# First microseconds: the first weights in two transfers, parameters on ScalarE's queue, part of the rounding on VectorE, x's first blocks in two PSUM buffers

## The chip, the cores and the metric

One core of one Trainium2 chip. The metric is the device time of one launch in microseconds (us). Engines: PE = TensorE, ACT = ScalarE, DVE = VectorE, POOL = GpSimd, SP = SyncE (it issues most DMA transfers here).

## The reference

A stack of four transformer-like layers, all in fp32, on x of 256 tokens by 1024 channels. What matters here is the very first step:

```python
def rms_norm(x, g):
    xf = x.astype(jnp.float32)
    y = xf * lax.rsqrt(jnp.mean(xf * xf, axis=-1, keepdims=True) + RMS_EPS)
    return (y * g.astype(jnp.float32)).astype(x.dtype)
...
    h = rms_norm(x, norm_mix_pre[layer])
    h = neighbourhood_attention(h, na_w_qkv[j], na_w_o[j], na_rpb[j])   # first: qkv = h @ w_qkv
```

Behind it come the output projection, a SwiGLU layer, dilated attention with a second SwiGLU layer, and twice a block of SwiGLU, four mixers (gated linear attention, forgetting attention, state space, short convolution) and SwiGLU. Nearly all the work is products with weight matrices of 1024 rows or columns.

## The kernel before, in words

The whole set of weights is laid out as a list of pieces, `w_all[m]`, each 128 partitions by 2048 columns (1 MB). SyncE fetches piece after piece into three raw buffers (`raw`). Each product is made in three fp32r products: ScalarE rounds the raw piece to fp32r (`wh`, the high part), VectorE subtracts (`wl` = raw - `wh`, the low part), and x is split in the same way into `xh` and `xl`. TensorE then adds `xh*wh`, `xl*wh` and `xh*wl` in PSUM. Low parts are ready later than high parts, so each piece's low products come last.

x comes in token rows and is needed with channels on the partitions. `turn(s, t, q)` does this for step s, token half t (128 tokens) and channel half q (four blocks of 128 channels). TensorE transposes four blocks of 128x128 into one PSUM buffer and signals once, behind the fourth (line 426, in `pe_program`). ScalarE waits for the signal and scales each block by the norm's gain, which is a column of the parameters `PR`, into `xh` (L1260). VectorE waits for ScalarE's fourth block and makes the four low parts `xl` (L1811). The factor of the norm itself is applied to the products later. The gains are in `PR`, which holds all small parameters (104 KB), and ScalarE waits for it before its first block.

At the start the values' projection of the first layer runs first (`values_start`), since its columns are in pieces 0 to 3. Piece 0 is treated apart: it comes in two transfers, columns 0 to 1023 (`s_first`) and 1024 to 2047 (`s_raw[0]`), and is rounded and subtracted in four pieces of 512 columns (`first_high`, L1238, and `first_low`, L1791). The issue order by hand is, on SyncE's queue: the identity (for transposes), the parameters, the first 1024 columns, x's second token half (512 KB), the second 1024 columns, pieces 1 and 2. On ScalarE's queue: x's first token half in two transfers of 256 KB, then the load of an activation table. TensorE waits for the identity, then does 7 filler transposes (`warm`), then `turn(0, 0, 0)`, `turn(0, 0, 1)`, 5 fillers, and `values_start`: the high products of channel block 0 for token half 0 (4 matmuls of 512 columns: `xh` with two column halves, `xl` with two), `turn(0, 1, 0)`, the low products of block 0 (2), high (4) and low (2) for token half 1, then block 1's (8 high), `turn(0, 1, 1)`, its 4 low ones, and piece 1. ScalarE's order is turn, first rounding (2), turn, turn, second rounding (2), piece 1. VectorE's is turn, first subtraction (2), turn, turn, second subtraction (2), piece 1. Each engine works in program order, and its waits are on semaphores.

Of the kernel before, what the change touches and what calls it, by code (L numbers as in the profile page):

```python
# [171 lines left out]
def build(nc, w_all, x_in, w_gu, cst, dist, prm, post, rpb, out):  # L172
    ctx = ExitStack()
    with ctx:
# [75 lines left out]
        s_first = signal("s_first", 16)  # L250
# [102 lines left out]
        def sp_program(e):  # L353
# [17 lines left out]
            q.on.dma_start(PR[:, :], prm).then_inc(*s_prm.up(0))  # L371
            q.on.dma_start(raw[0][:, 0:1024], w_all[0, :, 0:1024]).then_inc(*s_first.up(0))
# [37 lines left out]
        def pe_program(e):  # L410
# [10 lines left out]
            def turn(s, t, q):  # L421
                b = xbank(s, t, q)
                claim(b)
                t_.wait_ge(*(s_x[t][q * (1 - t)].of(0) if s == 0 else vx.of("x", s - 1, q, t)))
                for j in range(4):
                    k = t_.on.transpose(P[b][:, toks(j)], (xs if s else nx)[:, t, (4 * q + j) * 128:(4 * q + j + 1) * 128], ident)  # L426
                k.then_inc(*tx.up(("turn", s, t, q)))
                held[b] = [(vx, "lo", s, t, 4 * q + 3)]
# [325 lines left out]
            def values_start(banks):  # L754

                def high(m, i, t):
                    c = 2 * m + i
                    t_.wait_ge(*ax.of("hi", 0, t, c))
                    for x in (xh, xl):
                        for hf in range(2):  # L760
                            b = banks[t][hf]
                            if x is xl:
                                t_.wait_ge(*vx.of("lo", 0, t, c))
                            elif c == 0:
                                claim(b)
                            t_.wait_ge(*(hi.of(m) if m else hi.of(0, i, hf)))
                            mul(P[b][:, :], x[:, c, toks(t)], wh[m][:, (2 * i + hf) * 512:(2 * i + hf + 1) * 512],
                                x is xh and c == 0, False)
# [24 lines left out]
            def na():  # L793
                banks = ((2, 3), (4, 5))
                warm(2, 7)
                turn(0, 0, 0)
                turn(0, 0, 1)
                warm(2, 5)
# [421 lines left out]
        def act_program(e):  # L1220
# [13 lines left out]
            def first_high(i):  # L1234
                a.wait_ge(*(s_raw[0] if i else s_first).of(0))
                for hf in range(2):
                    n = slice(i * 1024 + hf * 512, i * 1024 + hf * 512 + 512)
                    a.on.activation(wh[0][:, n], raw[0][:, n], ACT.Copy).then_inc(*hi.up((0, i, hf), (0,)))  # L1238
                step["at"] = 1
# [14 lines left out]
            def turn(s, t, q):  # L1254
                b = xbank(s, t, q)
                name, l = GAINS[s]
                a.wait_ge(*tx.of("turn", s, t, q))
                for j in range(4):
                    c = 4 * q + j
                    a.on.activation(xh[:, c, toks(t)], P[b][:, toks(j)], ACT.Identity, bias=0.0,  # L1260
                                    scale=par(name, l, c)).then_inc(*ax.up(("hi", s, t, c)))
# [206 lines left out]
            def na():  # L1468
                turn(0, 0, 0)
                first_high(0)  # L1470
                turn(0, 0, 1)
# [276 lines left out]
            for h in range(2):  # L1748
                a.on.dma_start(nx[:, 0, halfs(h)], placed(0, halfs(h))).then_inc(*s_x[0][h].up(0))
            a.on.preload_act_table_set(LNEXP)  # L1750
# [12 lines left out]
        def dve_program(e):  # L1763
# [23 lines left out]
            def first_low(i):  # L1787
                for hf in range(2):
                    n = slice(i * 1024 + hf * 512, i * 1024 + hf * 512 + 512)
                    v.wait_ge(*hi.of(0, i, hf))  # L1790
# [14 lines left out]
            def turn(s, t, q):  # L1805
                b = xbank(s, t, q)
                name, l = GAINS[s]
                v.wait_ge(*ax.of("hi", s, t, 4 * q + 3))
                for j in range(4):
# [266 lines left out]
            def na():  # L2076
                turn(0, 0, 0)
# [514 lines left out]
        signals = s_raw + [s_first] + s_x[0] + s_x[1] + [s_ident, s_prm, s_cst, s_gu, s_dist] + s_rpb + [s_res, s_post] + s_out[0] + s_out[1]  # L2592
# [148 lines left out]
```

## Time and profile before

| | us |
|---|---|
| median of 3 runs | 1758.22 (1757.59 to 1758.23) |
| profiled execution, its own time | 1757.08 |
| its span, first to last instruction | 1755.3 |
| TensorE busy | 1747.8 |
| VectorE busy | 1226.1 |
| ScalarE busy | 987.8 |

The span leaves out what lies around the instructions (1757.08 less 1755.3). Busy time is a sum over an engine's instructions; ends of matmuls are modelled, so a busy TensorE is not one at its peak. Times in the trace count from the start of the span. 314.74 MB are moved, at 179 GB/s on average.

### The profile page before, as it was taken

What the parts mean: (1) busy time and instruction counts of PE and PEld (TensorE: products, weight loads), DVE (VectorE), ACT (ScalarE), POOL (GpSimd) and SP (SyncE); (2) the same over time, 40 slices, a digit from 0 to 9 for tenths busy, and PEclk for the clock granted to TensorE, in tenths of its full rate; (3) what the DMA queues carried; (4) which work ended last, traced back from release to release, by engine and by line L of the source; (5) the groups of instructions that cost most, each with busy time, mean ns of one, the idle gap of its engine ahead of it and who ended that gap; (6) DMA issues with size and microseconds to landing.
All of it is one profiled execution on the core that took longest, in us unless ns stands there. A gap on an engine that the chain in (4) does not pass through costs nothing.

```text
span 1755.3 us, 25579 instructions
## 1 busy us (share of the span) xinstructions
PE 1747.8 (100%) x10120; PEld 1499.3 (85%) x10120; DVE 1226.1 (70%) x1897; ACT 987.8 (56%) x1580; POOL 107.7 (6%) x191
## 2 busy tenths in 40 slices
PE   9999999999999999999999999999999999999999
PEld 7888888888888888888888888888888888888887
DVE  6877765667776777467756787775587648878763
ACT  6666554645555655365545666554565446656551
POOL 2000000701110000000001010000000001100000
PEclk9999999999999999999999999999999999999999
DMA  8435554554343455544454344555355534335552
GB/s 334 181 147 210 189 219 163 222 182 155 144 157 121 168 192 215 205 160 181 189 214 145 123 144 187 197 192 215 134 206 191 214 133 169 134 145 216 192 215 74
DMA packets 45353, 314.74 MB, mean 179 GB/s; under 512 B 5024, under 2 KB 5536, under 8 KB 8240
## 3 DMA queue, kind: packets, MB, share of 16 engines
q1 hardware_dynamic: 44912, 312.54, 47.8%
q8 instruction: 80, 1.31, 0.3%
q10 hardware_dynamic: 288, 0.52, 0.1%
q14 instruction: 41, 0.34, 0.0%
q0 software_dynamic: 32, 0.03, 0.0%
HBM read 312.03 MB, written 1.05 MB: 178 GB/s over the span
## 4 chain that ended last, share of the span: by engine, by line
PE 99%; DMA 0%; DVE 0%; ACT 0%; SPq 0%; issue 0%
PE P L419 96%; PE P L426 1%; PE P L718 1%; DMA raw<-w_all 0%; ACT xx L1260 0%; PE P L1058 0%; PE P L620 0%; PE P L1138 0%; DVE xx L1811 0%; PE P L1004 0%; DVE xs L1831 0%; PE P L1081 0%; PE P L952 0%; ACT wh L1238 0%; PE P L942 0%
## 5 line engine op out<-in xcount | busy, mean ns | idle before, releaser
L1776 DVE TENSOR_TENSOR wl<-raw,wh 128x2048 fp32r<-128x2048 f32 x287 | 656.8, 2294 | 186.9 <-ACT wh L1232 167.7
L1232 ACT ACTIVATE wh<-raw 128x2048 fp32r<-128x2048 f32 x291 | 551.8, 1900 | 191.3 <-PE P L419 170.6
L419 PE MATMUL P<-xx,wh 128*128 128x512 f32 (+2 forms) x2800 | 652.1, 385 | 0.0
L419 PEld LDWEIGHTS P<-xx,wh 128*128 128x128 f32 (+1 forms) x2800 | 503.1, 188 | 97.9 <-issue 1.7
L419 PEld LDWEIGHTS P<-xx,wl 128*128 128x128 f32 x2688 | 344.3, 191 | 12.4
L419 PE MATMUL P<-xx,wl 128*128 128x256 f32 x2688 | 350.7, 283 | 0.0
L1361 ACT ACTIVATE ft<-P 128x256 f32<-128x256 f32 x240 | 90.2, 382 | 231.8 <-PE P L419 231.8
L419 PE MATMUL P<-wh,fhh 128*128 128x512 f32 x528 | 206.2, 390 | 0.0
L419 PE MATMUL P<-wh,fhl 128*128 128x512 f32 x528 | 205.5, 389 | 0.0
L419 PE MATMUL P<-wl,fhh 128*128 128x512 f32 x528 | 205.5, 389 | 0.0
L1939 DVE TENSOR_TENSOR fg<-P,ft 128x256 f32<-128x256 f32 x240 | 101.8, 424 | 121.9 <-ACT ft L1361 116.7
L419 PE MATMUL P<-wh,xx 128*128 128x512 f32 x544 | 173.9, 395 | 0.9 <-ACT wh L1238 0.5
L419 PEld LDWEIGHTS P<-wh,xx 128*128 128x128 f32 x544 | 102.0, 188 | 23.1 <-issue 0.9
L419 PEld LDWEIGHTS P<-wh,fhl 128*128 128x128 f32 x528 | 99.1, 188 | 20.7
L419 PEld LDWEIGHTS P<-wh,fhh 128*128 128x128 f32 x528 | 99.1, 188 | 20.2
L419 PEld LDWEIGHTS P<-wl,fhh 128*128 128x128 f32 x528 | 99.2, 188 | 20.1
L419 PE MATMUL P<-wl,xx 128*128 128x512 f32 x272 | 104.3, 391 | 0.0
L1260 ACT ACTIVATE xx<-P,PR 128x128 fp32r<-128x128 f32 x160 | 45.1, 372 | 77.1 <-PE P L426 77.1
L1811 DVE SCALAR_TENSOR_TENSOR xx<-P,PR,xx 128x128 fp32r<-128x128 f32 x160 | 44.7, 344 | 58.1 <-ACT xx L1260 58.0
L2492 POOL TENSOR_TENSOR ss<-ss 128x2 f32<-128x2 f32 x10 | 2.0, 195 | 1147.0 <-ACT fsj L1265 903.7
L419 PE MATMUL P<-wh,dxp 128*128 128x512 f32 x192 | 61.2, 394 | 0.0
L1959 DVE TENSOR_TENSOR fh<-fs,fg 128x256 f32<-128x256 f32 x120 | 51.1, 426 | 13.9 <-DVE fg L1939 0.9
(326 smaller groups left out, 1468.3 us busy)
## 6 DMA issues: line engine op xcount, KB each, us to landing
raw<-w_all SPq DMA_DIRECT2D x289, 1024.0 KB, 4.8
nB<-rpb SPq DMA_DIRECT2D x4, 512.0 KB, 6.4
raw<-w_all SPq DMA_DIRECT2D x2, 512.0 KB, 6.5
xs<-x_in SPq DMA_DIRECT2D x1, 1024.0 KB, 7.7
fgb<-post SPq DMA_DIRECT2D x2, 512.0 KB, 6.2
out<-xs SPq DMA_DIRECT2D x4, 256.0 KB, 2.0
C<-cst SPq DMA_DIRECT2D x1, 769.0 KB, 8.4
ntm<-x_in ACTq DMA_DIRECT2D x2, 256.0 KB, 3.8
```

The lines of the kernel that those rows point to most:

```text
L419: return t_.on.matmul(o, l, r, start=start, stop=stop, skip_group_check=True)
L426: k = t_.on.transpose(P[b][:, toks(j)], (xs if s else nx)[:, t, (4 * q + j) * 128:(4 * q + j + 1) * 128], ident)
L718: k = t_.on.transpose(P[b][:, toks(place[c])], pA[h][:, toks(c)], ident)
L1232: a.on.activation(o, i, ACT.Copy).then_inc(*hi.up((m,)))
L1260: a.on.activation(xh[:, c, toks(t)], P[b][:, toks(j)], ACT.Identity, bias=0.0, scale=par(name, l, c)).then_inc(*ax.up(("hi", s, t, c)))
L1361: a.on.activation(AF["ft"][:, z, :], P[fbanks(s, j)[z]][:, S:2 * S], ACT.Copy).then_inc(*af.up(("side", s, j, z)))
L1776: v.on.tensor_tensor(o, i, h.bitcast(F32), ALU.subtract).then_inc(*lo.up(m))
L1811: v.on.scalar_tensor_tensor(xl[:, c, toks(t)], P[b][:, toks(j)], par(name, l, c), xh[:, c, toks(t)].bitcast(F32), ALU.mult, ALU.subtract). ...
L1939: v.on.tensor_tensor(fg[:, j % 2, z * S:z * S + S], P[fbanks(s, j)[z]][:, 0:S], AF["ft"][:, z, :], ALU.add).then_inc(*vf.up(("sum", s, j, z)))
L1959: v.on.tensor_tensor(fh[:, j % 3, :], sj, gj[:, S:2 * S], ALU.mult).then_inc(*vf.up(("h", s, j)))
L2492: g.on.tensor_tensor(ss[:, 4:6], ss[:, 0:2], ss[:, 2:4], ALU.add).then_inc(*gx.up(("sum", s)))
```

## The change

- SyncE issues the first 1024 columns of piece 0 as two transfers of 512 columns with a signal each, directly behind the identity.
- The parameters are issued by ScalarE's queue, behind x's two transfers and ahead of the table load.
- VectorE rounds columns 0 to 511 with a `tensor_copy` as its first instruction and signals it on its own semaphore (`lo`, name "first"). ScalarE rounds columns 512 to 1023 and later the second half of the piece, as before.
- The first `turn` is made in two: blocks 0 and 1 in PSUM buffer 6, as before, blocks 2 and 3 in buffer 1, each with its own signal. ScalarE's rounding of columns 512 to 1023 stands between the two. On VectorE both stand ahead of the first subtraction.
- The second row of fillers has 2 transposes, not 5.

```diff
--- before.py
+++ after.py
@@ -247,7 +247,7 @@
         P = [ctx.enter_context(nc.psum_tensor(f"P{i}", [128, 512], F32)) for i in range(8)]
 
         s_raw = [signal(f"s_raw{i}", 16) for i in range(RAW)]
-        s_first = signal("s_first", 16)
+        s_first = [signal(f"s_first{h}", 16) for h in range(2)]
         s_x = [[signal(f"s_x0{h}", 16) for h in range(2)], [signal("s_x1", 16)]]
         s_ident, s_prm, s_cst, s_gu, s_dist = (signal(n, 16) for n in ("s_ident", "s_prm", "s_cst", "s_gu", "s_dist"))
         s_res = signal("s_res", 16)
@@ -368,8 +368,8 @@
                 q.on.dma_start(gb, post[POST[s]:POST[s] + 1, :].broadcast_to([128, D])).then_inc(*s_post.up(s))
 
             q.on.dma_start(C[:, 0:128], cst[:, 0:128]).then_inc(*s_ident.up(0))
-            q.on.dma_start(PR[:, :], prm).then_inc(*s_prm.up(0))
-            q.on.dma_start(raw[0][:, 0:1024], w_all[0, :, 0:1024]).then_inc(*s_first.up(0))
+            for h in range(2):
+                q.on.dma_start(raw[0][:, halfs(h)], w_all[0, :, halfs(h)]).then_inc(*s_first[h].up(0))
             q.on.dma_start(nx[:, 1, :], placed(1, slice(0, D))).then_inc(*s_x[1][0].up(0))
             q.on.dma_start(raw[0][:, 1024:], w_all[0, :, 1024:]).then_inc(*s_raw[0].up(0))
             for m in range(1, RAW):
@@ -418,14 +418,14 @@
             def mul(o, l, r, start, stop):
                 return t_.on.matmul(o, l, r, start=start, stop=stop, skip_group_check=True)
 
-            def turn(s, t, q):
-                b = xbank(s, t, q)
+            def turn(s, t, q, js=(0, 1, 2, 3), b=None):
+                b = xbank(s, t, q) if b is None else b
                 claim(b)
                 t_.wait_ge(*(s_x[t][q * (1 - t)].of(0) if s == 0 else vx.of("x", s - 1, q, t)))
-                for j in range(4):
+                for j in js:
                     k = t_.on.transpose(P[b][:, toks(j)], (xs if s else nx)[:, t, (4 * q + j) * 128:(4 * q + j + 1) * 128], ident)
-                k.then_inc(*tx.up(("turn", s, t, q)))
-                held[b] = [(vx, "lo", s, t, 4 * q + 3)]
+                k.then_inc(*tx.up(("turn", s, t, q, js)))
+                held[b] = [(vx, "lo", s, t, 4 * q + js[-1])]
 
             def factors(s, b=6):
                 claim(b)
@@ -763,7 +763,7 @@
                                 t_.wait_ge(*vx.of("lo", 0, t, c))
                             elif c == 0:
                                 claim(b)
-                            t_.wait_ge(*(hi.of(m) if m else hi.of(0, i, hf)))
+                            t_.wait_ge(*(hi.of(m) if m else hi.of(0, i, hf) if i or hf else lo.of("first")))
                             mul(P[b][:, :], x[:, c, toks(t)], wh[m][:, (2 * i + hf) * 512:(2 * i + hf + 1) * 512],
                                 x is xh and c == 0, False)
 
@@ -793,9 +793,10 @@
             def na():
                 banks = ((2, 3), (4, 5))
                 warm(2, 7)
-                turn(0, 0, 0)
+                turn(0, 0, 0, (0, 1))
+                turn(0, 0, 0, (2, 3), 1)
                 turn(0, 0, 1)
-                warm(2, 5)
+                warm(2, 2)
                 values_start(banks)
                 for m in range(2, 4):
                     tok(0, m, 2 * m, banks)
@@ -1232,8 +1233,8 @@
                 a.on.activation(o, i, ACT.Copy).then_inc(*hi.up((m,)))
 
             def first_high(i):
-                a.wait_ge(*(s_raw[0] if i else s_first).of(0))
-                for hf in range(2):
+                a.wait_ge(*(s_raw[0] if i else s_first[1]).of(0))
+                for hf in range(1 - i, 2):
                     n = slice(i * 1024 + hf * 512, i * 1024 + hf * 512 + 512)
                     a.on.activation(wh[0][:, n], raw[0][:, n], ACT.Copy).then_inc(*hi.up((0, i, hf), (0,)))
                 step["at"] = 1
@@ -1251,11 +1252,11 @@
                     for t in range(2):
                         a.wait_ge(*ax.of("sq", s, h, t))
 
-            def turn(s, t, q):
-                b = xbank(s, t, q)
+            def turn(s, t, q, js=(0, 1, 2, 3), b=None):
+                b = xbank(s, t, q) if b is None else b
                 name, l = GAINS[s]
-                a.wait_ge(*tx.of("turn", s, t, q))
-                for j in range(4):
+                a.wait_ge(*tx.of("turn", s, t, q, js))
+                for j in js:
                     c = 4 * q + j
                     a.on.activation(xh[:, c, toks(t)], P[b][:, toks(j)], ACT.Identity, bias=0.0,
                                     scale=par(name, l, c)).then_inc(*ax.up(("hi", s, t, c)))
@@ -1466,8 +1467,9 @@
                 post_end(s, dbanks(s))
 
             def na():
-                turn(0, 0, 0)
+                turn(0, 0, 0, (0, 1))
                 first_high(0)
+                turn(0, 0, 0, (2, 3), 1)
                 turn(0, 0, 1)
                 turn(0, 1, 0)
                 first_high(1)
@@ -1747,6 +1749,7 @@
 
             for h in range(2):
                 a.on.dma_start(nx[:, 0, halfs(h)], placed(0, halfs(h))).then_inc(*s_x[0][h].up(0))
+            a.on.dma_start(PR[:, :], prm).then_inc(*s_prm.up(0))
             a.on.preload_act_table_set(LNEXP)
             a.wait_ge(*s_ident.of(0))
             a.wait_ge(*s_prm.of(0))
@@ -1787,7 +1790,7 @@
             def first_low(i):
                 for hf in range(2):
                     n = slice(i * 1024 + hf * 512, i * 1024 + hf * 512 + 512)
-                    v.wait_ge(*hi.of(0, i, hf))
+                    v.wait_ge(*(hi.of(0, i, hf) if i or hf else lo.of("first")))
                     v.on.tensor_tensor(wl[0][:, n], raw[0][:, n], wh[0][:, n].bitcast(F32),
                                        ALU.subtract).then_inc(*lo.up((0, i, hf), (0,)))
                 step["at"] = 1
@@ -1802,11 +1805,11 @@
                 v.wait_ge(*mm.of("half", s - 1, 1, 1))
                 v.wait_ge(*ax.of("sq", s, 1, 1))
 
-            def turn(s, t, q):
-                b = xbank(s, t, q)
+            def turn(s, t, q, js=(0, 1, 2, 3), b=None):
+                b = xbank(s, t, q) if b is None else b
                 name, l = GAINS[s]
-                v.wait_ge(*ax.of("hi", s, t, 4 * q + 3))
-                for j in range(4):
+                v.wait_ge(*ax.of("hi", s, t, 4 * q + js[-1]))
+                for j in js:
                     c = 4 * q + j
                     v.on.scalar_tensor_tensor(xl[:, c, toks(t)], P[b][:, toks(j)], par(name, l, c),
                                               xh[:, c, toks(t)].bitcast(F32), ALU.mult,
@@ -2074,7 +2077,10 @@
                 post_end(s, gb, tmp, dbanks(s))
 
             def na():
-                turn(0, 0, 0)
+                v.wait_ge(*s_first[0].of(0))
+                v.on.tensor_copy(wh[0][:, halfs(0)], raw[0][:, halfs(0)]).then_inc(*lo.up("first"))
+                turn(0, 0, 0, (0, 1))
+                turn(0, 0, 0, (2, 3), 1)
                 first_low(0)
                 turn(0, 0, 1)
                 turn(0, 1, 0)
@@ -2589,7 +2595,7 @@
                 means(s + 2)
 
 
-        signals = s_raw + [s_first] + s_x[0] + s_x[1] + [s_ident, s_prm, s_cst, s_gu, s_dist] + s_rpb + [s_res, s_post] + s_out[0] + s_out[1]
+        signals = s_raw + s_first + s_x[0] + s_x[1] + [s_ident, s_prm, s_cst, s_gu, s_dist] + s_rpb + [s_res, s_post] + s_out[0] + s_out[1]
         signals += [mm, tx, ta, th, hi, ax, aa, af, ah, lo, vx, va, vf, vh, gx, ga, gh]
         for program in (sp_program, act_program, dve_program, pool_program, pe_program):
             program(Still())
```

## Rows read from the trace of the kernel before

**Rows 1.** The page, busy time of TensorE (us, share of the span, instructions)

```profile
PE 1747.8 (100%) x10120; PEld 1499.3 (85%) x10120; DVE 1226.1 (70%) x1897; ACT 987.8 (56%) x1580; POOL 107.7 (6%) x191
```

**Rows 2.** The page, chain that ended last, shares of the span by engine

```profile
PE 99%; DMA 0%; DVE 0%; ACT 0%; SPq 0%; issue 0%
```

**Rows 3.** Waits of PE, whole span: engine, line, releaser: us, times, longest

```profile
PE P L752 <- DMA C<-cst: 2.5, 1, 2.5
PE P L419 <- ACT wh L1238: 0.5, 1, 0.5
PE P L419 <- DVE xx L1811: 0.4, 1, 0.4
```

**Rows 4.** Chain of the first 60 us: start, us, what

```profile
1.64 5.61 DMA raw<-w_all
...
9.91 1.16 ACT xx L1260 x4
...
11.09 0.36 DVE xx L1811
...
11.50 3.02 PE P L419 x12
```

**Rows 5.** Timeline of the issues: start, us, engine and line, operation, count

```profile
0.73 1.27 ACTq L1749 DMA_DIRECT2D ntm<-x_in  x2
1.18 0.42 SPq L371 DMA_DIRECT2D PR<-prm  x1
...
1.64 0.46 SPq L372 DMA_DIRECT2D raw<-w_all  x1
...
2.15 0.64 SPq L373 DMA_DIRECT2D ntm<-x_in  x1
```

**Rows 6.** DMA issues of 0.7 to 4.0 us: count, KB, us to landing

```profile
ntm<-x_in ACTq DMA_DIRECT2D x1, 256.0 KB, 3.7
...
PR<-prm SPq DMA_DIRECT2D x1, 104.0 KB, 3.4
...
raw<-w_all SPq DMA_DIRECT2D x1, 512.0 KB, 5.6
...
ntm<-x_in ACTq DMA_DIRECT2D x1, 256.0 KB, 3.9
...
ntm<-x_in SPq DMA_DIRECT2D x1, 512.0 KB, 6.8
...
raw<-w_all SPq DMA_DIRECT2D x1, 1024.0 KB, 9.1
```

**Rows 7.** Timeline of ScalarE

```profile
5.72 1.15 ACT L1260 ACTIVATE xx<-P,PR 128x128 fp32r<-128x128 f32 x4 [2.40 <-PE P L426]
...
7.27 1.15 ACT L1238 ACTIVATE wh<-raw 128x512 fp32r<-128x512 f32 x2 [0.40 <-DMA raw<-w_all]
...
12.64 1.92 ACT L1232 ACTIVATE wh<-raw 128x2048 fp32r<-128x2048 f32 x1 [0.54 <-DMA raw<-w_all]
```

**Rows 8.** Timeline of TensorE

```profile
2.55 1.76 PE L752 MATMUL P<-C 128*128 128x128 f32 x7 [2.55 <-DMA C<-cst]
...
4.49 1.98 PE L426 MATMUL P<-C,ntm 128*128 128x128 f32 x8 [0.18 <-DMA ntm<-x_in]
...
9.28 0.60 PE L426 MATMUL P<-C,ntm 128*128 128x128 f32 x4
...
15.73 3.82 PE L419 MATMUL P<-wh,xx 128*128 128x512 f32 x16
```

**Rows 9.** Timeline of VectorE, its first six instructions

```profile
7.02 1.12 DVE L1811 SCALAR_TENSOR_TENSOR xx<-P,PR,xx 128x128 fp32r<-128x128 f32 x4 [7.02 <-ACT xx L1260]
...
8.06 1.28 DVE L1791 TENSOR_TENSOR wl<-raw,wh 128x512 fp32r<-128x512 f32 x2
```

**Rows 10.** VectorE's groups of 0 to 60 us: busy, mean ns | idle before

```profile
L2089 DVE COPY nrb<-rb 128x256 f32<-128x256 f32 x1 | 0.7, 706 | 0.0
...
L2088 DVE TENSOR_SCALAR nrb<-rb 128x256 f32<-128x256 f32 x1 | 0.3, 294 | 0.0
```

## The prediction

> **What bounds the kernel now.** I read the page first. TensorE is busy for the whole span, 1747.8 of 1755.3 us [rows 1], and the chain that ended last is 99% TensorE [rows 2]. So almost nothing but TensorE's own work counts, and the change leaves that work as it is, apart from three filler transposes. Then the waits of TensorE over the whole run: beside 2.5 us for the identity at the start there are 0.5 us for rounded weights, 0.4 us for a low part of x, and nothing of size later [rows 3]. So there is no later stall that could swallow or enlarge a shift of the first microseconds. What the change can be worth is decided where TensorE stops waiting for the last time. The chain of the first 60 us gives that place: weights land at 7.25 (1.64 + 5.61), ScalarE rounds them, TensorE turns x's second token half from 9.28 on [rows 8], ScalarE scales it from 9.91 on, VectorE makes its low part at 11.09, TensorE goes on at 11.50 and does not stop again [rows 4]. I call 11.50 the last wait. A step that comes early ahead of it and does not move it is worth nothing.
>
> **The transfers.** Issues take their queue 0.4 to 0.6 us each. ScalarE's queue issues x's two halves of the first 128 tokens at 0.73 and about 1.38, ending at 2.00; SyncE's issues the parameters at 1.18, the first weights at 1.64, x's second token half at 2.15 [rows 5]. From issue to landing they take 3.7 and 3.9 us (x's halves: 4.43 and 1.38 + 3.9 = 5.28), 3.4 (parameters: 4.58), 5.6 (first weights: 7.25), 6.8 (second token half: 8.95) and 9.1 (piece 1: about 12.6) [rows 6]. After the change SyncE loses one issue (parameters, 0.42) and gains one (weights, about 0.46), so everything behind on its queue starts as before, and the bytes ahead of it are the same. The first 512 columns of the weights are issued at 1.18 and are half as large. They land between 4.9 (3.7 after issue, as the first 256 KB of x) and 7.25. The second 512 columns are issued at 1.64, with the identity, x, half the weights and perhaps the parameters before them. If the parameters' 104 KB come first, they land at 7.25 as now. If not, then earlier by 104/512 of the 1.97 us between x's landing at 5.28 and the weights' at 7.25, which is 0.4 us: 6.85. I take the middle, 7.05. The parameters become third on ScalarE's queue, at 2.00. From below 2.00 + 3.4 = 5.4; from above 2.00 + 6.8 = 8.8, the longest of the neighbours. I take the middle between x's 5.28 and the weights' 7.25: 6.3, against 4.58 now.
>
> **ScalarE.** Four scalings of x take 1.15 us, so they start 0.26 apart; two roundings take 1.15, 0.54 apart [rows 7]. x's first two blocks wait only for two transposes: TensorE starts at 4.49 and issues them 0.21 apart [rows 8], so they could be scaled from about 5.3 instead of 5.72. But they now wait for the parameters: 6.35, and ScalarE is free after two at 6.87. The gain of 0.4 us turns into a wait of 0.6, which costs nothing as long as ScalarE is free when the weights land, that is, while the parameters land before 6.48 (7.05 less two scalings, 0.52, and a pick-up of 0.05). Then the one rounding that stays here runs 7.07 to 7.70, the second pair of x's blocks starts at 7.61 and ends at 7.61 + 0.26 + 0.37 = 8.24, and x's blocks 4 to 7 run from 8.13 to 9.26. For the second token half ScalarE waits for TensorE, whose transposes wait for the landing at 8.95. They started at 9.28 before, behind matmuls that waited for the second rounding; those matmuls now end at about 8.6. So they start at 8.97, ScalarE at 9.60 instead of 9.91, and its fourth block is ready at 10.7 instead of 11.05. This is the only gain on the old chain: 0.3 us.
>
> **VectorE.** The new copy of 128x512 is not in the trace. From below it costs the 0.3 us that an operation with a constant takes for half that width, from above twice the slow 128x256 copy of 0.71, 1.4 us; I take 0.68, as the subtraction of this size (two in 1.28, 0.60 apart) [rows 9, 10]. If its weights land by 5.9 it is over by 6.6, and VectorE has nothing else before 6.9, as it now has nothing before 7.02: hidden, and at 1.4 us it is nearly so, since it idles again from 7.7 to 8.2. It frees ScalarE of 0.54 us. But behind it the order has changed. Before, the subtractions for the first weights began at 8.06, right behind the low parts of four blocks [rows 9]. Now the low parts of blocks 2 and 3 stand ahead of the subtractions on VectorE, and they wait for ScalarE's blocks, which stand behind the rounding, which waits for the weights: they start at 8.24 + 0.06 = 8.30. Then 2 x 0.26 = 0.52, two subtractions 2 x 0.60 = 1.20, blocks 4 to 7 4 x 0.26 = 1.04: 8.30 + 2.76 = 11.06 for the low part of the second token half. Before: 11.09. VectorE's queue takes the place of ScalarE's 10.7, and the 0.3 us won there is not collected.
>
> **TensorE.** Two PSUM buffers instead of one: the claim of the second is against a low part done at 9 us for a turn at 14.4, so it costs nothing. First matmul at about 6.8 instead of 8.05, the second at 7.75, subtractions' matmuls at 9.5 and 10.1. All of it ends before 11 and only adds idle time. After the last wait TensorE has the same work. What stands behind it as a floor: the 16 matmuls with piece 1's rounded weights start at 15.73 [rows 8], and its rounding starts at 12.64 on a transfer and takes 1.92 [rows 7], so it is ready at 14.56, and no shift beyond 1.17 us can pass.
>
> **The sum.** 11.06 against 11.09 is -0.03 us, to be read as none; with the weights at 7.25 it is +0.17, at 6.85 it is ended by ScalarE's 10.7 and gives -0.3. The profiled execution took 1757.08 us, 1.78 more than its span; the median of the runs is 1758.22, 1.14 above it, and the three differ by 0.64. I forecast 1758.2 and count 0.2%, 3.5 us, as what a measurement of this kernel tells from no change.
>
> **TensorE's clock.** The granted clock stands at full speed, 2.4 GHz, everywhere, yet the early transposes start 0.21 us apart up to 7.1 and 0.11 apart at 9.28 [rows 8]. I read that as the lower of the two levels, 1.2 GHz, in the first microseconds, not shown in the clock's row; the engine had worked almost without a gap from 2.55 to past 7 before it rose. Now the fillers end at about 6.6, and then come some eight matmuls in five microseconds. The Trainium skill, "TensorE: Matmul & The Clock Gate", Part 4 (PE-mode transpose), says that transposes do not count as TensorE being busy the way matmuls do. By that rule the dropped fillers cost nothing and the earlier first matmul would help. The trace speaks against it: at 9.28 only four matmuls had run, and the transposes were already at the fast spacing.
>
> **Rivals.** (A) *Transfers land earlier* (smaller ones, other order): weights by 6.7 and the second token half before 8.7. For it: the first weights are issued 0.46 earlier. Against: the same bytes are ahead. It gives 0.3 to 1.17 us, 1757.6. (B) *Parameters late*: they become the bound from a landing at 6.48 on, and from there each 0.1 us shifts ScalarE, VectorE and the last wait by 0.1. For it: they stand behind 512 KB of x on one queue and beside the weights on the other. At 7.25, with the weights, it is 7.25 + 0.57 - 7.05 = 0.77 late: 1759.0; at 8.8 it is 2.3 late: 1760.5. (C) *The clock rises later*, the slow side's worst: TensorE pauses too long after the shortened fillers and is at 1.2 GHz when the dense work begins at 11.5. Before, the climb took from 2.55 to between 7.1 and 9.28, 4.6 to 6.7 us. As long again at half rate loses half of it, 2.3 to 3.4 us: about 1761. It decides only if the low level outlasts 11.5; the slack before covers it. For it: fewer fillers, a gap at 6.6. Against: the engine kept the fast spacing at 9.28 after a wait of 0.5 us, and the wait of 0.4 us before 11.50 did it no harm [rows 3]. (D) *The split brings nothing*: the first 512 columns land with the rest at 7.25, VectorE's copy (0.68) ends at 7.95, still before its low parts of blocks 2 and 3 at 8.3; it gives the forecast's time, within 0.3.
>
> **Chances.** Forecast 0.50 (its own range 1757.9 to 1758.6), A 0.17, B 0.18, C 0.10, D 0.05. Only the edge of C with B on top passes 3.5 us: slower 0.03. No case gives a gain of 3.5 us; 0.02 for what I do not see; same 0.95. The range leaves out C (0.10) and some of B's and A's ends: 1757.0 (the floor of 1.17) to 1760.2.
>
> **What would show it.** Right: TensorE's first real matmul before 7, its last wait still near 11.5 and for VectorE's x, no idle time of VectorE between 8.3 and 11.4, ScalarE's first scaling at about 6.3 on the parameters, ScalarE idle before 9.6. Wrong: the last wait before 11.2 or after 11.8; weights' second half landing outside 6.85 to 7.25; transposes at about 9 still 0.21 apart and matmuls after 11.5 over 0.23 apart.

## The result, and the profile after

The changed kernel takes 1760.86 us in the median of 20 runs (1760.19 to 1761.38), the kernel before 1757.39 us in 20 runs beside it (1756.90 to 1758.94). The ratio is 1.0018, with a 95% interval of 1.0012 to 1.0024: 3.5 us slower. The profiled execution took 1761.38 us, 4.30 more than the one of before, with a span of 1759.6. It is the slowest of the 20 runs, 0.5 above their median, and the profiled one of before (1757.08) is 0.3 under its own, so the two traces show 0.8 us more than the medians do. One run of the kernel before, beside e9 to e12, took 6168.8 us and is left out everywhere.

The page of the changed kernel, busy time and the chain's shares by engine. TensorE's work is as before [rows 1, 2], but for three fillers. It is busy for 1.2 us more, from transposes and matmuls at a lower clock (below); the other 3.1 us of the longer span are waiting:

```profile
PE 1749.0 (99%) x10117; PEld 1500.0 (85%) x10117; DVE 1226.0 (70%) x1898; ACT 987.1 (56%) x1579; POOL 107.5 (6%) x191
...
PE 99%; DMA 0%; DVE 0%; ACT 0%; ACTq 0%; issue 0%; DVEq 0%
```

TensorE's waits (us in total, times, longest). The 2.4 us for x and the 1.8 us at the first real matmul are new [rows 3]:

```profile
PE P L426 <- DMA ntm<-x_in: 2.4, 1, 2.4
PE P L419 <- DVE wh L2081: 1.8, 1, 1.8
```

The chain of the first 60 us (start, us, what). Where the first weights stood [rows 4], the parameters stand now, for 8.32 us. The dense stretch, which began at 11.50, hangs on them and begins at 15.76 (inside the last line, which the view merges over the wait):

```profile
2.05 8.32 DMA PR<-prm
...
10.45 0.44 DVE wh L2081
...
11.03 2.26 PE P L419 x4
...
14.14 4.73 PE P L419 x16
```

The issues in their order (count, KB, us to landing), to be laid beside [rows 6]. x's halves land at 4.03 and at 1.4 + 6.2 = 7.6 (5.28 before), the weights' halves at 6.2 and 8.9 (7.25), the parameters at 2.05 + 8.3 = 10.4 (4.58), x's second token half at 10.55 (8.95):

```profile
ntm<-x_in ACTq DMA_DIRECT2D x1, 256.0 KB, 3.3
...
raw<-w_all SPq DMA_DIRECT2D x1, 256.0 KB, 5.0
...
ntm<-x_in ACTq DMA_DIRECT2D x1, 256.0 KB, 6.2
...
raw<-w_all SPq DMA_DIRECT2D x1, 256.0 KB, 7.3
...
PR<-prm ACTq DMA_DIRECT2D x1, 104.0 KB, 8.3
...
ntm<-x_in SPq DMA_DIRECT2D x1, 512.0 KB, 8.4
```

ScalarE and VectorE (start, us, line, operation, count, idle time before and who ended it). Both start at 10.45: ScalarE on the parameters, and VectorE's copy with it, though the copy's weights were there at 6.2. ScalarE had waited 6.47 us. VectorE's program begins with a wait for the parameters too (line 2466), ahead of the new copy. VectorE's idle time before its second token half, 0.37 us at 15.36, is a wait for ScalarE, which waited for TensorE at 14.18:

```profile
10.45 0.63 ACT L1261 ACTIVATE xx<-P,PR 128x128 fp32r<-128x128 f32 x2 [6.47 <-DMA PR<-prm]
10.45 0.43 DVE L2081 CAST wh<-raw 128x512 fp32r<-128x512 f32 x1 [10.45 <-DMA PR<-prm]
...
12.67 1.28 DVE L1794 TENSOR_TENSOR wl<-raw,wh 128x512 fp32r<-128x512 f32 x2
...
14.18 1.14 ACT L1261 ACTIVATE xx<-P,PR 128x128 fp32r<-128x128 f32 x4 [1.04 <-PE P L426]
...
15.36 1.13 DVE L1814 SCALAR_TENSOR_TENSOR xx<-P,PR,xx 128x128 fp32r<-128x128 f32 x4 [0.37 <-ACT xx L1261]
```

TensorE. The four transposes at 13.09 start 0.21 us apart, where those of [rows 8] at 9.28 started 0.11 apart, and of the four real matmuls at 14.79 the first two start 0.43 us apart, where the dense stretch of before has 0.23 [rows 8] (the other two follow the last wait, at 15.76):

```profile
7.67 1.12 PE L426 MATMUL P<-C,ntm 128*128 128x128 f32 x4 [2.39 <-DMA ntm<-x_in]
...
11.03 2.26 PE L419 MATMUL P<-wh,xx 128*128 128x512 f32 x4 [1.81 <-DVE wh L2081]
...
13.09 1.05 PE L426 MATMUL P<-C,ntm 128*128 128x128 f32 x4
...
14.79 1.77 PE L419 MATMUL P<-wh,xx 128*128 128x512 f32 x4
```

### The profile page after: what moved, and what is told of

Same layout as the page of the kernel before. It is cut to its first block, busy times and chain, and to the rows that moved or that the text cites. A ratio compares the mean times of both kernels' runs of the same rounds, so it can differ in the third digit from the quotient of the medians.

```text
span 1759.6 us, 25574 instructions
## 1 busy us (share of the span) xinstructions
PE 1749.0 (99%) x10117; PEld 1500.0 (85%) x10117; DVE 1226.0 (70%) x1898; ACT 987.1 (56%) x1579; POOL 107.5 (6%) x191
## 4 chain that ended last, share of the span: by engine, by line
PE 99%; DMA 0%; DVE 0%; ACT 0%; ACTq 0%; issue 0%; DVEq 0%
PE P L419 96%; PE P L426 1%; PE P L718 1%; DMA PR<-prm 0%; PE P L620 0%; PE P L1139 0%; PE P L1059 0%; ACT xx L1261 0%; DVE xx L1814 0%; PE P L1005 0%; DVE xs L1834 0%; ACTq L1751 0%; PE P L953 0%; PE P L1082 0%; PE P L943 0%
## 5 line engine op out<-in xcount | busy, mean ns | idle before, releaser
L1375 ACT ACTIVATE fs<-fg 128x256 f32<-128x256 f32 x120 | 49.7, 415 | 19.9 <-DVE fg L1955 16.6
```

The source lines that it names most:

```text
L1375: a.on.activation(fs[:, j % 2, :], fg[:, j % 2, 0:S], ACT.Silu).then_inc(*af.up(("s", s, j)))
```

## The experiments

"Before" in each is the kernel before, run beside it on the same chip: 1757.38 to 1757.45 us. Landings are counted from the start of the span, each in one trace. How far a landing moves by itself is seen in e2, e3, e8, e9 and e11, whose first transfers are the same: the parameters take 3.5 to 4.1 us, x's second half 4.0 to 4.5, the first 512 columns of the weights 4.4 to 5.1. A difference of 0.7 us or less between two traces says little.

**e1: only the parameters moved.**

```diff
-            q.on.dma_start(PR[:, :], prm)...          # SyncE, behind the identity
+            a.on.dma_start(PR[:, :], prm)...          # ScalarE, behind x's two transfers
```

> The kernel before, with the one edit that the parameters are issued third on ScalarE's queue. Theory 1 (the place behind x on that queue is what delays the parameters): they land 8 to 10.4 us into the span, ScalarE's first scaling waits for them, TensorE's dense stretch begins 3 to 4 us late and the time rises by 2.5 to 4 us. Theory 2 (the split of the weights into 2 KB rows slows all transfers): the parameters land by 6.5, the time rises by less than 1 us.

Measured: 1761.93 us, 4.5 above before (ratio 1.0025, 1.0014 to 1.0035). This one line costs at least as much as the whole change (the intervals overlap), and 0.5 more than the expectation's upper end: beside the late parameters, the second token half is turned 0.21 us per block at 13.66. Landings (x's second half, x's second token half, parameters), 7.7, 9.0 and 9.9:

```profile
ntm<-x_in ACTq DMA_DIRECT2D x1, 256.0 KB, 6.3
...
ntm<-x_in SPq DMA_DIRECT2D x1, 512.0 KB, 7.4
...
PR<-prm ACTq DMA_DIRECT2D x1, 104.0 KB, 7.9
```

Theory 1 holds. The weights here are one transfer with rows of 4 KB, so the split (theory 2) is not needed for the delay.

**e2: the changed kernel without that move.**

```diff
+            q.on.dma_start(PR[:, :], prm)...          # back behind the identity
-            a.on.dma_start(PR[:, :], prm)...
```

> The changed kernel, with the parameters back on SyncE's queue directly behind the identity. Theory 1: they land at about 4.6 again, the first real matmul is before 7.5, and the time is that of the kernel before or up to 0.5 us less. Theory 2: the weights' halves and x's second token half still land 1.5 us later than in the kernel before, and the time stays 1.5 to 2 us above it. Theory 3 (fewer fillers, lower clock at the dense stretch) gives at least 1 us above the kernel before, with matmuls more than 0.4 us apart past 10 us.

Measured: 1758.14 us, 0.7 above before (1.0003, 0.9993 to 1.0012), 2.7 below the changed kernel. The parameters land at 4.9, the first matmul is at 6.96. The timeline is the forecast's, step by step:

```profile
6.39 0.43 DVE L2081 CAST wh<-raw 128x512 fp32r<-128x512 f32 x1 [6.39 <-DMA raw<-w_all]
...
7.94 0.63 ACT L1240 ACTIVATE wh<-raw 128x512 fp32r<-128x512 f32 x1 [1.88 <-DMA raw<-w_all]
...
9.65 1.28 DVE L1794 TENSOR_TENSOR wl<-raw,wh 128x512 fp32r<-128x512 f32 x2
...
10.85 2.15 DVE L1814 SCALAR_TENSOR_TENSOR xx<-P,PR,xx 128x128 fp32r<-128x128 f32 x8
...
12.28 0.30 PEld L420 LDWEIGHTS P<-wh,xx 128*128 128x128 f32 x2 [0.77 <-DVE xx L1814]
```

VectorE rounds at 6.39, ScalarE rounds its half at 7.94 when it lands, VectorE's subtractions start at 9.65, its second token half follows without idle time, and the last wait ends at 12.28. That is 4.4 us behind the weights' landing at about 7.9, as the forecast's chain has it (7.05 to 11.06 for VectorE, plus 0.4 for TensorE's pick-up). The weights' second half landed 0.65 later than the whole did before, and it is issued 0.5 us later. Theory 3's case came by half: the median is not 1 us above.

**e3: only the split of the weights.**

```diff
+            for h in range(2):
+                q.on.dma_start(raw[0][:, halfs(h)], w_all[0, :, halfs(h)])...(s_first[h])
```

> The kernel before, with the one edit that the first 1024 columns of the weights come as two transfers with a signal each, on the queue's old place behind the parameters; ScalarE rounds both. Theory 1: landings move by under 0.3 us, the time is the same within 0.3 us. Theory 2: the second half, x's second token half and piece 1 land 1 us or more later than before, and the time rises by 1 to 1.7 us.

Measured: 1757.43 us against 1757.45 (0.9999, 0.999 to 1.0008). The split alone costs nothing and brings nothing that can be measured. The expectation had landings within 0.3 us, and that was a miss: in the trace x's second half lands at 5.8 (5.28 before) and piece 1 at 13.4 (12.6), with a last wait at 11.90, not 11.50.

**e4: 14 fillers in the changed kernel.**

```diff
-                warm(2, 2)
+                warm(2, 14)
```

> The changed kernel with 14 fillers, not 2, behind the turns, so that TensorE works from x's last turn to about the first real matmul. The parameters still land at about 10.4. If the low clock costs time (theory 3), the matmuls from 11 on are 0.23 us apart and the time falls by 0.4 to 1.2 us against the changed kernel. If the late parameters alone set the time, it moves by less than 0.2 us.

Measured: 1760.97 us, 0.1 above the changed kernel: no gain in the median. Yet in its trace the clock is up when it counts:

```profile
11.49 1.17 PE L419 MATMUL P<-wh,xx 128*128 128x512 f32 x4
...
12.50 0.60 PE L426 MATMUL P<-C,ntm 128*128 128x128 f32 x4
```

The four transposes at 12.50 start 0.11 apart, four matmuls at 11.49 take 1.17 us, and the last wait is at 14.98, not 15.76. Of these 0.8 us, 0.3 are the parameters' landing (ScalarE starts at 10.12, not 10.45), and 0.5 come behind it, where the transposes are faster and VectorE has no idle time before x's second token half. This profiled execution is 0.66 us shorter than that of the changed kernel, but the medians don't show it. How often the changed kernel runs into the lower clock late was not counted. Open.

**e5: the parameters on SyncE's queue, behind the first weights.**

```diff
-            q.on.dma_start(PR...); q.on.dma_start(raw[0][:, 0:1024]...)
+            q.on.dma_start(raw[0][:, 0:1024]...); q.on.dma_start(PR...)
```

> The kernel before, with the parameters on SyncE's queue still, but behind the first weights (512 KB) and not ahead of them. Theory S (what starves the parameters is ScalarE's queue: the transfer engines share between the two queues by packets, and SyncE's packets are larger and more): on SyncE's queue they land directly behind the weights, at 6.8 to 7.5, and the time rises by 0.7 to 1.3 us. Theory O (the order of issue is all: whatever is issued behind x and the weights waits for the whole backlog): they land at 8 or later and the time rises by over 2 us. By either, x's second half of the first 128 tokens lands at 7 or later, not at 5.3, since the weights are now issued 0.46 earlier beside it.

Measured: 1759.62 us, 2.2 above before. x's second half lands at 7.1, the parameters at 7.44. The landing is theory S's; the time is not (it had 0.7 to 1.3). In the trace the chain runs through x's second half, its turn and the five fillers to the first matmuls, at 9.3, so the time is not the parameters' alone. The profiled execution (1758.68) was this kernel's fastest:

```profile
PR<-prm SPq DMA_DIRECT2D x1, 104.0 KB, 5.8
```

**e6: parameters as in e1, and SyncE holds back what is behind the weights.**

```diff
             (SyncE, behind the first weights)
+            q.wait_ge(*s_prm.of(0))
             q.on.dma_start(nx[:, 1, :], ...)
```

> The parameters third on ScalarE's queue as in the first experiment, and SyncE waits for their landing before it issues x's second token half and all behind it. Theory S: what delays them is SyncE's transfers that are issued after them, so they land by 7, 3 us earlier than in the first experiment. Theory O: only what was issued before counts, so they land at 9 to 10 again. The time is no measure here, since x's second token half and piece 1 come 3 to 5 us later: 2 to 6 us above the kernel before.

Measured: the parameters land at 7.3, not 9.9; 1759.66 us, 2.3 above before and 2.3 *below* e1, although x's second token half is now issued at 7.36, 5.7 us later than in e1:

```profile
PR<-prm ACTq DMA_DIRECT2D x1, 104.0 KB, 5.3
```

So 2.6 us of e1's delay come from transfers of SyncE's queue other than the first weights: x's second token half, which e1 issues at 1.64, ahead of the parameters (2.03), and the rest, from 2.32 on, behind them. What stands behind is enough by itself: the changed kernel has the same bytes issued ahead of the parameters as e6 (the weights in two transfers), all else of SyncE's from 2.15 on behind them, and they land at 10.4. On SyncE's own queue (e5), with the same transfers behind, they land at 7.44.

**e7: the parameters first on ScalarE's queue.**

```diff
+            a.on.dma_start(PR[:, :], prm)...
             for h in range(2): a.on.dma_start(nx[:, 0, halfs(h)]...)
```

> The changed kernel with the parameters first on ScalarE's queue, ahead of x's two transfers. They should land at 3.5 to 4.5. Then VectorE's order sets the last wait by the forecast's formula, 4.4 us behind the landing of the weights' second half: with it at 7.5 to 9 the dense stretch starts at 12 to 13.4, 0.5 to 2 us above the kernel before. If x's second half lands after 8 (it is now third on its queue), ScalarE's blocks 4 to 7 are late too.

Measured: 1761.55 us, 4.2 above before (expected: 0.5 to 2). The parameters are there at 3.1, and x, issued 0.45 us later, is starved in their place: its first half lands at 1.2 + 7.9 = 9.1, its second at 11.0. My expectation for x was a miss:

```profile
PR<-prm ACTq DMA_DIRECT2D x1, 104.0 KB, 2.4
...
ntm<-x_in ACTq DMA_DIRECT2D x1, 256.0 KB, 7.9
```

**e8: e2 with VectorE's subtractions in their old place.**

```diff
-                turn(0, 0, 0, (2, 3), 1)
                 first_low(0)
+                turn(0, 0, 0, (2, 3), 1)
```

> The changed kernel with the parameters back on SyncE's queue (second experiment) and one more edit: on VectorE the first two subtractions stand ahead of the low parts of blocks 2 and 3, as they stood before the change. If VectorE's new order is what left that version 0.4 us (in the trace) to 0.7 us (in the runs) behind the kernel before, the last wait comes 0.4 to 0.5 us earlier relative to the landing of the weights' second half (3.9 us behind it, not 4.4) and the time falls to within 0.3 us of the kernel before. If not, it stays at 0.5 to 0.8 above.

Measured: 1758.32 us, but its runs go from 1756.67, under the fastest of before, to 1760.22. The time fell into neither case. The profiled one is of the lower clock, and its last wait comes 4.8 us behind the weights, not 3.9; TensorE turns x's second token half 0.21 us per block at 9.89, and ScalarE gets it at 10.98:

```profile
9.89 1.05 PE L427 MATMUL P<-C,ntm 128*128 128x128 f32 x4
...
10.98 1.14 ACT L1262 ACTIVATE xx<-P,PR 128x128 fp32r<-128x128 f32 x4 [1.05 <-PE P L427]
```

**e9: e8 with 7 fillers, not 2.**

```diff
-                warm(2, 2)
+                warm(2, 7)
```

> The changed kernel with the parameters on SyncE's queue, VectorE's first subtractions ahead of the low parts of blocks 2 and 3, and 7 fillers, not 2, behind the turns. Theory C (the early pause of TensorE leaves it at the lower clock and that is what holds the e8 version back): the matmuls from 8.4 on are 0.23 us apart, x's second token half is turned by 9.2, the last wait is at 11.3 to 11.8, and the time is 0.8 to 1.2 us below e8, that is 0.3 us below the kernel before to 0.1 above. Without theory C it stays 0.9 us above the kernel before.

Measured: 1757.45 us, 0.9 below e8 (run apart from it), and level with before's 1757.38 (1.0001, 0.9992 to 1.001). The second row of fillers starts its transposes 0.11 us apart, the first row, of as many, 0.21 apart, and no real matmul has run in between. The transposes of x's second token half are 0.11 apart at 9.32, the last wait ends at 11.54, 3.7 us behind the weights' landing at 7.84:

```profile
2.71 1.76 PE L753 MATMUL P<-C 128*128 128x128 f32 x7 [2.71 <-DMA C<-cst]
...
6.37 1.00 PE L753 MATMUL P<-C 128*128 128x128 f32 x7
...
8.50 0.69 DVE L1794 TENSOR_TENSOR wl<-raw,wh 128x512 fp32r<-128x512 f32 x1 [0.79 <-ACT wh L1240]
...
9.32 0.60 PE L427 MATMUL P<-C,ntm 128*128 128x128 f32 x4
...
10.05 2.21 DVE L1814 SCALAR_TENSOR_TENSOR xx<-P,PR,xx 128x128 fp32r<-128x128 f32 x8 [0.34 <-ACT xx L1262]
...
11.54 0.30 PEld L420 LDWEIGHTS P<-wh,xx 128*128 128x128 f32 x2 [0.87 <-DVE xx L1814]
```

**e10: only the three fillers taken from the kernel before.**

```diff
-                warm(2, 5)
+                warm(2, 2)
```

> The kernel before with the one edit that the second row of fillers has 2, not 5. Theory C: TensorE stops at about 6.9, in some executions the lower clock lasts past 9, and the median rises by 0.2 to 1 us with a wider spread. If the three fillers are of no use, the time is the same within 0.2 us.

Measured: 1758.26 us, 0.9 above before (1.0003, 0.9994 to 1.0012). Its 11 runs fall into two groups, 1757.3 to 1757.6 (four) and 1758.2 to 1758.5 (seven). The profiled one is of the second: four matmuls take 2.08 us, not 1.39, and ScalarE waits until 11.33, not 9.91:

```profile
8.36 2.08 PE L419 MATMUL P<-wh,xx 128*128 128x512 f32 x4 [1.29 <-ACT wh L1238]
...
10.23 1.05 PE L426 MATMUL P<-C,ntm 128*128 128x128 f32 x4
...
11.33 1.14 ACT L1260 ACTIVATE xx<-P,PR 128x128 fp32r<-128x128 f32 x4 [1.56 <-PE P L426]
```

The mechanism is theory C's: the turn comes 0.95 us later (the weights 0.3 later), the last wait 1.4. The median by itself proves nothing, since its interval includes no change, and the kernel before has long runs too: 45 of its 138 in all are at 1758.0 or above, 6 of the 31 beside this one. Over all runs it is a matter of how often: with 2 fillers (e2, e8, e10) 20 of 31 are at 1758.0 or above, with 5 or 7 (e3, e9, e11, e13, e14) 10 of 54.

**e11: e2 with 7 fillers (e9 with the changed kernel's order on VectorE).**

```diff
-                warm(2, 2)
+                warm(2, 7)
```

> The second experiment's kernel (the changed one with the parameters on SyncE's queue) with 7 fillers. Beside e9 it differs by VectorE's order alone: by the forecast's chain it has its last wait 4.4 us behind the landing of the weights' second half, e9 3.6 to 3.9, so it is 0.4 to 0.8 us slower than e9. If VectorE's order is of no account, the two are the same.

Measured: 1757.75 us, 0.3 above e9, with the last wait at 12.21 against 11.54 and the weights' second half landed at nearly the same time (ScalarE's rounding at 7.87 and 7.84). VectorE's order costs what its queue says in the trace; in the median the intervals overlap.

**e12: e1 with SyncE's first transfers in rows of 2 KB.**

```diff
+                for h in range(4):
+                    q.on.dma_start(raw[m][:, halfs(h)], w_all[m, :, halfs(h)])...   # and so for all before it
```

> The first experiment's kernel (parameters third on ScalarE's queue), with all of SyncE's first transfers cut into 256 KB with rows of 2 KB each, where they had rows of 4 and 8 KB. If the engines share between the queues by packets of one row, ScalarE's queue gets a larger part of the bytes: the parameters land at 7.5 to 9, not at 9.9, and x's second half before 7. If they share otherwise (by transfer, or ScalarE's queue is served last while SyncE's has work), they land at 9.5 or later.

Measured: 1761.58 us, 4.2 above before; x's second half at 1.4 + 6.1 = 7.5, the parameters at 2.04 + 7.5 = 9.5, 0.4 earlier than in e1, no more than what traces differ by. The width of SyncE's rows has little to do with it, the more so as the narrower transfers are also issued later (x's second token half from 2.15, not 1.64).

**e15: e1, with the weights issued only behind the identity's landing.**

```diff
+            q.wait_ge(*s_ident.of(0))
             q.on.dma_start(raw[0][:, 0:1024], ...)
```

> The first experiment's kernel (parameters third on ScalarE's queue), and SyncE waits for the identity's landing (2.5 to 3) before it issues the first weights. If a transfer's landing goes mostly by what was issued ahead of it on either queue, x's second half is back at 5.0 to 5.6 (7.6 in the first experiment), and the parameters, with only x and the identity ahead, land at 5.5 to 7.5, not at 9.9, though SyncE's queue is full behind them. If instead ScalarE's third transfer is always starved by SyncE's, the parameters stay at 9 or later. The weights land at about 8; the time is 0.5 to 2 us above the kernel before by the first, 3.5 or more by the second.

Measured: 1760.31 us, 2.9 above before (the weights land at 3.04 + 6.2 = 9.2; the expectation had 8 and a time 0.5 to 2 above). x's second half is at 4.9, the parameters at 6.6, with SyncE's queue filling from 3.04 on, 1.0 behind them. TensorE's fillers end at 7.0, it waits 3.07 us, and the matmuls at 10.04 are at the lower clock again:

```profile
ntm<-x_in ACTq DMA_DIRECT2D x1, 256.0 KB, 3.5
...
PR<-prm ACTq DMA_DIRECT2D x1, 104.0 KB, 4.6
...
6.26 0.71 PE L752 MATMUL P<-C 128*128 128x128 f32 x5
...
10.04 2.08 PE L419 MATMUL P<-wh,xx 128*128 128x512 f32 x4 [3.07 <-ACT wh L1238]
```

**e13 and e14: 4 KB of the parameters ahead of the weights, the rest behind**, in the kernel before (e13) and in e9 (e14). ScalarE and GpSimd wait for the rest where they first need it.

```diff
-            q.on.dma_start(PR[:, :], prm)...
+            q.on.dma_start(PR[:, 0:8], prm[:, 0:8])...      # and PR[:, 8:] behind raw[0][:, 1024:]
```

> The kernel before, with the parameters cut in two: their first 8 columns (4 KB, the gains that the first scaling needs) keep the old place ahead of the first weights, the other 100 KB are issued by SyncE behind the second half of piece 0. If what protects x's second half in the kernel before is the issue time that the parameters take on SyncE's queue, x's second half stays at 5.0 to 5.4 and the weights land up to 0.3 us earlier: the time is 0 to 0.4 us below the kernel before. If it is the bytes, x's second half lands 1 us or more later.

> The same cut of the parameters in the e9 version (split weights, VectorE's part of the rounding, x's first blocks in two PSUM buffers, VectorE's subtractions first, 7 fillers). The last wait comes 3.6 to 3.9 us behind the weights' second half; with that 0.2 us earlier the time is 0.1 to 0.4 us below both kernels, which five rounds may not tell from none.

Measured: 1757.30 and 1757.44 us against 1757.43 (intervals 0.9988 to 1.0006 and 0.999 to 1.0008): no version beats the kernel before by what can be measured. In e13 x's second half lands at 1.4 + 4.8 = 6.2, 0.9 later than before, with the same issue times. That would say that the bytes of the parameters protect it; but e14, with the same cut, has it at 1.4 + 3.6 = 5.0, 0.4 earlier than e9. What the bytes do is open:

```profile
ntm<-x_in ACTq DMA_DIRECT2D x1, 256.0 KB, 4.8
...
ntm<-x_in ACTq DMA_DIRECT2D x1, 256.0 KB, 3.6
```

In e14's trace the last wait of the start ends at 11.30, 0.2 earlier than before, and the gain is given back at 47 us, in the chain:

```profile
11.30 2.99 PE P L422 x12
...
47.27 0.27 DVE npA L2040
47.54 0.34 DVE nq L2104
...
54.91 0.44 PE P L721 x4
```

TensorE waits for VectorE's probabilities and queries of the first attention there, and its transposes stand at 54.91, where the chain of the kernel before has them at 54.40. Why VectorE is late is open: ScalarE rounds piece 1 from 13.32, not 12.64, but at 40.58 VectorE is level with the kernel before (40.54), and 0.38 us behind only after the subtraction there, which took 2.70 us, not 2.36. In e9 the transposes that follow are as early as before, and the matmuls behind them, on VectorE's queries, 0.25 later (55.01 against 54.76).

None of these runs has the copy on VectorE or the two PSUM buffers alone. e9 has both, with the split, and is level with the kernel before.

## Why the prediction was wrong

*The step that failed* is the parameters' landing: "I take the middle between x's 5.28 and the weights' 7.25: 6.3". It was 10.4, outside even the bound of 8.8. A middle between neighbours' landings supposes that a transfer waits for what was issued ahead of it, whatever its queue. That held on SyncE's queue: behind the first weights the parameters land at 7.44 (e5). On ScalarE's it did not. With the same bytes ahead and SyncE held back they land at 7.3 (e6), with SyncE's next transfers going out beside and behind them at 9.9 (e1) and 10.4 (changed kernel); with SyncE's whole bulk 1 us behind, and only x and the identity ahead, at 6.6 (e15). My upper bound took the neighbour that was slowest, but that neighbour was measured on SyncE's queue, in another order. In the kernel before, the parameters had the place with the least ahead.

*The same step for x.* I had x's second half unchanged at 5.28; it landed at 7.6. The weights, issued at 1.17 instead of 1.64, now go beside it: with them at 3.04 (e15) it is at 4.9, with them at 1.17 (e1, otherwise the same) at 7.7. It did not set the end here, since ScalarE waited longer for the parameters.

*And for the weights.* Their second half, put at 7.05 with 6.85 to 7.25 as bounds, landed at 1.6 + 7.3 = 8.9. The late parameters hid it. With parameters in time, the forecast's own 4.4 us behind it would have given a last wait at 13.3, 1.8 us late; e2, where it landed at 7.9, has 12.28.

*Rival B was the right mechanism*, with a chance of 0.18 and too small a price. Its rule, that from 6.48 on each 0.1 us shifts the last wait by 0.1, holds: ScalarE starts at 10.45, the effective landing is 10.45 + 0.52 = 10.97, and with the 4.0 us from there to VectorE's second token half, the forecast's chain gives 14.97 against 11.09, 3.9 us late. Measured 15.36; the missing 0.4 is VectorE's wait of 0.37 us for blocks turned at the lower clock (rival C). 15.76 - 11.50 = 4.26 us at the last wait, and 4.30 between the profiled executions. e4 confirms the share of C: faster transposes there give back about that much. The range's upper end, 1760.2, took in only part of B's price (up to 1760.5) and none of C's, and the median is 0.7 above it. It would have been further above had the base been right: the sum began from 1758.2, the median of three runs, and 20 runs have 1757.39.

*What held.* TensorE stops for the last time for VectorE's low part of the second token half, and a loss there comes out whole at the end (4.26 of 4.30). For gains I was wrong: "no later stall that could swallow" was read from waits that TensorE does not have in the kernel before; with 0.2 us gained, e14 has one at 47 us in its one trace. VectorE's queue takes ScalarE's place (e2 4.4, e11 4.3 us behind the weights; e9 with the old order: 3.7). The split is worth nothing by itself (rival D, e3). The forecast for the change without the moved parameters, "no change", is e2 (+0.7) and, with 7 fillers, e11 (+0.4), neither clear of zero.

*VectorE's copy* was over-priced at 0.68: 0.43 us. The Trainium skill, "VectorE: DVE Perf Modes", "The perf-mode tier table", gives a fp32 copy within SBUF twice the rate of a subtraction of two tensors; 0.43 against the 0.68 of a subtraction, fixed cost included, agrees. The forecast also had it start when its weights land, and left out the wait for the parameters ahead of it: it ran at 10.45, not by 5.9. Neither changed the end: the first matmul took its columns at 11.03, and the second waited until 11.64 for ScalarE's rounding.

*The fillers.* In the medians e10 alone costs 0.9 us, and 7 fillers in place of 2 give 0.9 (e8 to e9) and 0.4 (e2 to e11); none of these is clear of zero alone, and the counts of long runs, at 1758.0 or above (20 of 31 against 10 of 54) are the better evidence. I had the mechanism as rival C, but as an accident at 11.5 us with a price of 2.3 to 3.4. It costs less and comes more often: the turn of x's second token half at about 9 us is already on the chain, and at half rate it comes 1 us late. So "the slack before covers it" was wrong. The fillers are all transposes, and in e9 they reach the faster spacing before the first real matmul. That speaks against the rule of the Trainium skill weighed in the forecast ("TensorE: Matmul & The Clock Gate", Part 4). The trace of before, with four matmuls ahead of its fast transposes, could not tell by itself.

## What to carry to other kernels

Moving a small transfer to another queue "because it has room" is not free: price it by what is in flight on all queues when it is issued, and by what will be issued behind it, not by neighbours of its size. The tiny transfer that everything waits for belongs ahead of the bulk, and each issue time of the bulk that moves forward takes from what others have in flight. When a chain is tightened, write down each engine's program order behind it: here the early start was paid back by low parts that now stood ahead of the subtractions. Where a kernel's first matmuls matter, fillers are part of the chain, and they show in how often the runs are long, so read the spread of the runs beside one trace. And before a landing in one trace is explained, see how far it moves between traces of kernels with the same transfers.

## What the runs showed of the hardware

- A 104 KB transfer took from issue to landing 2.4 us (first on its queue, e7), 3.4 to 4.1 (in its old place: before, e2, e3, e8 to e11), 4.6 (e15), 5.3 (e6), 5.8 (e5), 7.5 (e12), 7.9 (e1), 8.0 (e4) and 8.3 (changed kernel), by its place and by what was in flight. The Trainium skill, "DMA: Bandwidth & Descriptors", "Queues, rings and completion order", says that each engine takes turns between the queues packet by packet. By it, ScalarE's queue would get its turns however much waits on SyncE's, and would still share the engines with it; no run here shows the turns. e6 against e1 shows 2.6 us of delay from the other queue, and narrower rows there gave back 0.4 at most (e12). What sets the share of ScalarE's queue was not found.
- The granted clock reads 1.00 in stretches where transposes are 0.21 us apart and where they are 0.11 apart. The level can be read from the spacing only. In e9 the spacing went from 0.21 to 0.11 while TensorE had done nothing but transposes, and a wait of 0.92 us did not take it back (three matmuls in 0.96 us at 8.52). In e15 it had gone to 0.11 too, and behind a wait of 3.07 us four matmuls took 2.08 us.
- The runs of e10 fall into two groups 0.9 us apart. The kernel before has both as well, with fewer in the upper one (45 of 138 at 1758.0 or above).
